# One transformer layer with paged decode: cached keys stored channel first, with homes of their own beside the values

## What is computed

```
z = h @ w_in                                   # 13 tiles of up to 512 columns, for all 320 tokens
# indexer: scores of the 8 new tokens of a sequence against its 1032 keys
ik_all = concat([cache_ik[page_table].reshape(db, 1024, 64), ik], 1)
scores = sum_h( relu(iq_h @ ik_all.T / 8) * w_h );  idx = top_k(scores, 256)
# attention of the same tokens over the chosen keys
s = q @ k_sel.T / 8;  p = softmax(s);  o = p @ v_sel     # k and v from cache_k, cache_v by page
# retention with a state per sequence; then three projections; then a mixture of 32 experts
x = x + gt1 * (merged @ w_o);   x = x + gt2 * moe(h2)
```

## Time and profile before

| | |
|---|---|
| median of 3 runs | 1524.77 us (1523.85 to 1530.13) |
| profiled execution | 1522.9 us, of which span 1520.9 us |
| PE busy | 1416.1 us, 93% |
| DVE, ACT, POOL busy | 465.1, 234.1, 81.1 us |
| HBM traffic | 483 MB read, 4 MB written |
| granted TensorE clock, mean | 0.978 of full |
| share of PE, of DMA in the chain that ended last | 34%, 35% |

### The profile page before, as it was taken

The page is one execution under the profiler, slowest core; times in us unless marked ns, Lnnn a source line. Parts: engine busy times, 40 slices in busy tenths (PEclk is TensorE's granted clock), DMA queues, the critical chain, the costliest instruction groups (busy, mean ns, idle before and its releaser), DMA issues.

```text
span 1520.9 us, 16634 instructions
## 1 busy us (share of the span) xinstructions
PE 1416.1 (93%) x6667; PEld 580.3 (38%) x6667; DVE 465.1 (31%) x993; ACT 234.1 (15%) x420; POOL 81.1 (5%) x71
## 2 busy tenths in 40 slices
PE   4899999998898779999999999999999999999993
PEld 2454555564443343333333333333333333333331
DVE  4233597653221241221211311221221131122124
ACT  1020232114202121111111111111111011011111
POOL 0200510231000020000000000000000000000000
PEclk8999999999999969999999999999999999999998
DMA  7532316437755439999999999999999999999991
GB/s 276 184 125 72 138 58 164 166 118 258 276 200 194 175 136 382 429 427 427 427 430 429 428 429 428 428 429 429 429 428 428 428 428 430 429 428 429 428 427 65
DMA packets 74042, 488.18 MB, mean 321 GB/s; under 512 B 6312, under 2 KB 16872, under 8 KB 48272
## 3 DMA queue, kind: packets, MB, share of 16 engines
q1 hardware_dynamic: 71488, 475.01, 76.4%
q0 software_dynamic: 1792, 10.49, 2.0%
q10 hardware_dynamic: 720, 2.10, 0.4%
HBM read 483.46 MB, written 4.08 MB: 321 GB/s over the span
## 4 chain that ended last, share of the span: by engine, by line
DMA 35%; PE 34%; DVE 2%; ACT 1%; issue 1%; POOL 0%; POOLq 0%; DVEq 0%; SPq 0%; ACTq 0%
DMA ring<-in_w_gate_up 35%; PE ps L1408 15%; PE ps L1449 5%; PE ps L865 2%; PE ps L866 2%; PE ps L1355 2%; PE ps L1386 1%; PE ps L869 1%; PE ps L1293 1%; PE ps L1401 1%; PE ps L1310 1%; PE ps L1316 0%; PE ps L1431 0%; PE ps L1363 0%; PE ps L1390 0%
## 5 line engine op out<-in xcount | busy, mean ns | idle before, releaser
L1408 PE MATMUL ps<-ring,z 128*64 128x512 f32 x2048 | 451.1, 595 | 20.9 <-DMA ring<-in_w_gate_up 20.9
L1408 PEld LDWEIGHTS ps<-ring,z 128*64 128x64 f32 x2048 | 142.2, 137 | 327.6 <-issue 277.8
L1449 PE MATMUL ps<-ring,z 128*64 128x512 f32 x1024 | 226.0, 594 | 0.0
L1985 DVE TENSOR_SCALAR actT<-ps 128x512 f32<-128x512 f32 x32 | 22.1, 692 | 647.3 <-PE ps L1408 647.3
L1449 PEld LDWEIGHTS ps<-ring,z 128*64 128x64 f32 x1024 | 72.0, 137 | 149.4 <-issue 145.1
L884 PE MATMUL ps<-ring,actT 128*128 128x512 f32 (+1 forms) x208 | 107.2, 597 | 3.3 <-DMA ring<-in_w_in 3.3
L885 PE MATMUL ps<-ring,actT 128*128 128x512 f32 (+1 forms) x208 | 104.7, 585 | 0.0
L1355 PE MATMUL ps<-z,actT 128*64 128x512 f32 x384 | 88.6, 596 | 1.3 <-DVE actT L1937 1.3
L1386 PE MATMUL ps<-z,aT 128*128 128x512 f32 x128 | 66.2, 619 | 1.7 <-ACT z L803 1.2
L1958 DVE TENSOR_TENSOR z<-z,ps 128x512 f32<-128x512 f32 x64 | 44.0, 688 | 61.3 <-PE ps L1386 61.2
L791 ACT ACTIVATE actT<-actT 128x512 f32<-128x512 f32 x32 | 20.1, 628 | 259.5 <-DVE actT L1985 259.5
(11 more groups left out here) (322 smaller groups left out, 1304.2 us busy)
## 6 DMA issues: line engine op xcount, KB each, us to landing
ring<-in_w_gate_up SPq DMA_DIRECT2D x128, 2048.0 KB, 23.4
ring<-in_w_down SPq DMA_DIRECT2D x64, 2048.0 KB, 20.6
ring<-in_w_ada SPq DMA_DIRECT2D x12, 2048.0 KB, 8.7
ring<-in_w_in SPq DMA_DIRECT2D x12, 2048.0 KB, 7.8
ring<-in_w_branch_b SPq DMA_DIRECT2D x2, 2048.0 KB, 10.6
ring<-in_w_out SPq DMA_DIRECT2D x2, 2048.0 KB, 10.7
ring<-in_state SPq DMA_DIRECT2D x8, 256.0 KB, 7.7
ret_sample<-ring SPq DMA_DIRECT2D x8, 256.0 KB, 7.5
```

Of the source, the lines that this page charges most:

```text
L1408: done = nc.tensor.matmul(bank(q // 2)[64 * (q % 2):64 * (q % 2) + 64, :], lhs, ring3[k // 2][:, (k % 2) * 2048 + q * BANK:(k % 2) * 2048 ...
L1449: done = nc.tensor.matmul(bank(2)[64 * q:64 * q + 64, :], lhs, ring3[4 + k // 4][:, (k % 4) * D + q * BANK:(k % 4) * D + (q + 1) * BANK], ...
```

## The change

The host now lays the caches out as `cache_kT` (page, channel, key), `cache_v` and `cache_ik` (page, channel, key), and passes the page numbers. Index keys are gathered by page, straight into `ikT`, 32 gathers of 64 KB in place of 8 of 256 KB. Attention keys are loaded by page from SP (sequences 0 to 5 during z tiles 10 to 12, sequence 6 in the attention) and from ACT (sequence 7): each page is a register load from `pt`, then a DMA of 64 KB with a row of 512 bytes for each channel. Keys and values have separate homes. POOL gathers the values alone, 512 KB a sequence, all after the last `new_state`. The transposes of keys and their copies go. The first pair's scores come before the wait for the rows' copies and the mask, and the modulation tile of a round follows directly on the values of the round before.

```diff
-        ikn = [scr(5332 + 1024 * i, 1024)... for i in range(PAIRS)]
-        kv_z = [z3[:, t, CRQ:CRG] for t in range(3)]
-        kv = [kv_z[0], kv_z[1], scr(5332, 2048), kv_z[2], scr(7380, 2048), scr(11476, 2048), scr(9428, 2048), kv_z[0]]
-        kT = [scr(2060, KEYS), scr(15316, KEYS)]
+        k_homes = [z3[:, 0, CRQ:CRG], z3[:, 1, CRQ:CRG], scr(5332, 2 * PAST), z3[:, 0, CRQ:CRG]]
+        v_homes = [z3[:, 2, CRQ:CRG], scr(11476, 2 * PAST), scr(7380, 2 * PAST), scr(9428, 2 * PAST)]
+        kT = [k_homes[b // 2][:, PAST * (b % 2):PAST * (b % 2 + 1)] for b in range(DB)]
...
+        def load_keys(q, b, first=0, last=NPAGES):
+            for n in range(first, last):
+                page = q.value_load(pt[0:1, b * NPAGES + n:b * NPAGES + n + 1], min_val=0, max_val=NPOOL - 1)
+                q.dma_start(kT[b][:, n * PAGE:(n + 1) * PAGE],
+                            a["cache_kT"][bass.ds(page, 1)].rearrange("a d s -> (a d) s")).then_inc(keys_here[b // 2], 16)
...
         @block.sync
-            load_z_tiles(10, 13)
+            sp.wait_ge(pr_here, 32)
+            load_z_tiles(10, 11)
+            sp.wait_ge(r_o, 1)
+            load_keys(sp, 0)
+            load_keys(sp, 1)
+            load_z_tiles(11, 12)
+            sp.wait_ge(r_o, 2)
+            load_keys(sp, 2)
+            load_keys(sp, 3)
+            load_z_tiles(12, 13)
             sp.wait_ge(retp_done, 1)
             sp.dma_start(a["ret_prompt"]...)
+            sp.wait_ge(r_o, 3)
+            load_keys(sp, 4)
+            load_keys(sp, 5)
             load_modulation(17, 4)
...
             load_modulation(19, 6)
+            sp.wait_ge(ssc2_done, 1)
+            load_keys(sp, 6)
             load_modulation(20, 7)
...
         @block.gpsimd
-            pool.wait_ge(h_done, 2)
-            for b in range(DB):
-                nc.gpsimd.indirect_dma_start(ikn[b // 2][:, :, b % 2, :].rearrange("p n d -> p (n d)"), None, rows,
-                                             bass.IndirectOffsetOnAxis(ap=irow[:, b:b + 1], axis=0)).then_inc(gathered[b // 2], 16)
+            pool.wait_ge(tile_done, 4)
+            for i in range(PAIRS):
+                for n in range(NPAGES):
+                    at = DB + i * NPAGES + n
+                    nc.gpsimd.indirect_dma_start(ikT[i][:, n * PAGE:(n + 1) * PAGE], None, rows,
+                                                 bass.IndirectOffsetOnAxis(ap=irow[:, at:at + 1], axis=0)).then_inc(gathered[i], 16)
...
             pool.wait_ge(ns_mm, 4)
-            gather_keys_values(3)
-            gather_keys_values(5)
-            pool.wait_ge(st_out[0], 64)
-            gather_keys_values(4)
-            pool.wait_ge(st_out[1], 64)
-            gather_keys_values(6)
-            pool.wait_ge(spv_done, 1)
-            gather_keys_values(7)
+            for b in range(DB):
+                if b in (4, 6):
+                    pool.wait_ge(st_out[b // 2 - 2], 64)
+                gather_values(b)
...
         @block.scalar
-            keys_out(0)
-            keys_out(1)
             for i in range(PAIRS):
-                if i + 1 < PAIRS:
-                    keys_out(2 * i + 2)
                 act.wait_ge(smx_done, i + 1)
...
-                if i + 1 < PAIRS:
-                    keys_out(2 * i + 3)
+                if i < 2:
+                    load_keys(act, 7, 4 * i, 4 * i + 4)
...
         @block.tensor
             for i in range(2):
-                prompt_steps(i, 0, 4)
-                index_transpose(2 * i)
-                prompt_steps(i, 4, KT)
-                index_transpose(2 * i + 1)
+                prompt_steps(i, 0, KT)
                 sample_steps(i)
...
             def sample_scores(i):
-                pe.wait_ge(kt_done, 4 * i + 4)
+                pe.wait_ge(keys_here[i], 32 * NPAGES)
...
             def sample_values(i):
                 pe.wait_ge(spt_done, i + 1)
+                for b in (2 * i, 2 * i + 1):
+                    pe.wait_ge(gathered[b], 16 * NPAGES + 16 if b < PAIRS else 16)
...
-            key_transpose(0)
-            key_transpose(1)
             sample_scores(0)
             for i in range(PAIRS):
-                if i + 1 < PAIRS:
-                    key_transpose(2 * i + 2)
                 if i:
                     pe.wait_ge(spt_done, i)
+                else:
+                    pe.wait_ge(rows_done, 6)
                 modulation_tile(17 + i, 3)
-                if i + 1 < PAIRS:
-                    key_transpose(2 * i + 3)
                 if i:
                     sample_rows(i - 1)
                 sample_prob_transposes(i)
...
         @block.vector
-            for i in range(PAIRS):
-                for h in range(2):
-                    dve.wait_ge(ikt_tr, 2 * i + h + 1)
-                    nc.vector.tensor_copy(ikT[i].rearrange("p (s n) -> p n s", n=8)[:, 4 * h:4 * h + 4],
-                                          bank(3 + 2 * (i % 2) + h).rearrange("p (n s) -> p n s", n=4)).then_inc(ikt_done, 1)
...
-            sample_top(1)
+            sample_top(2)
             new_state(2)
-            sample_top(1)
+            sample_top(2)
             new_state(3)
-            sample_top(2)
```

More of the change, by code:

```diff
@@ L284, in kern @@
         sa_tr, so_done, r_done, r_zero = sem("sa_tr"), sem("so_done"), sem("r_done"), sem("r_zero")
+        keys_here = [sem(f"keys_here{i}") for i in range(PAIRS)]
         gathered = [sem(f"gathered{b}") for b in range(DB)]
@@ L695, in _ @@
                     act.wait_ge(rows_tr, 2 * t + i + 1)
+                    b, at = ((5, 0), (6, 0), (7, 0), (3, 0), (4, 0), (4, 4 * NS))[2 * t + i]
                     nc.scalar.activation(rT[:, 4 * i:4 * i + 4, t * P:t * P + n],
-                                         bank((5, 0, 3)[t] + i).rearrange("p (k n) -> p k n", k=4)[:, :, 0:n],
+                                         bank(b)[:, at:at + 4 * n].rearrange("p (k n) -> p k n", k=4),
                                          ACT.Copy).then_inc(rows_done, 1)
[L700 to L708, removed]
             def sample_rows_out(i):
@@ L899, in sample_steps @@
                 last.then_inc(tile_done, 1)
-            def index_transpose(i):
-                pe.wait_ge(gathered[i], 32)
-                for h in range(2):
-                    if i >= 2:
-                        pe.wait_ge(ikt_done, 2 * (i - 2) + h + 1)
-                    for n in range(4):
-                        for j in range(2):
-                            last = nc.tensor.matmul(bank(3 + 2 * (i % 2) + h)[64 * j:64 * j + 64, n * P:(n + 1) * P],
-                                                    ikn[i][:, 4 * h + n, j, :], ident, start=True, stop=True)
-                    last.then_inc(ikt_tr, 1)
             def key_and_index_query_transposes():
                 pe.wait_ge(ikd_done, 1)
-                pe.wait_ge(ikt_done, 2 * PAIRS)
                 for t in range(3):
@@ L960, in sample_dots @@
                     pe.wait_ge(iw_done, 1)
+                pe.wait_ge(gathered[i], 16 * NPAGES)
                 for k in range(2):
@@ L1160, in _ @@
             for t in range(3):
[L1161 to L1162 removed]
                 n = TOK[t]
[L1164 to L1179 removed]
+                for i in range(2):
+                    if t == 0:
+                        pe.wait_ge(ns_done, 3)
+                    if t == 1 and i:
+                        pe.wait_ge(ns_done, 4)
+                    b, at = ((5, 0), (6, 0), (7, 0), (3, 0), (4, 0), (4, 4 * NS))[2 * t + i]
+                    for k in range(4):
+                        last = nc.tensor.transpose(bank(b)[:, at + k * n:at + (k + 1) * n],
+                                                   h2[0:n, t, (4 * i + k) * P:(4 * i + k + 1) * P], ident[0:n, 0:n])
+                    if t < 2:
+                        last.then_inc(rows_tr, 1)
+            last.then_inc(rows_tr, 2)
             def modulation_tile(n, b):
@@ L1201, in sample_scores @@
                     pe.wait_ge(z_done, NZT)
-                    pe.wait_ge(masks_done, 1)
-                    pe.wait_ge(rep_done, DB)
-                    pe.wait_ge(vnew_here, 16 * DB)
-                for k, w in ((0, BANK), (1, BANK), (2, DS)):
+                blocks = ((0, BANK), (1, BANK), (2, DS))
+                for k, w in blocks:
                     if i and k == 2:
@@ L1209, in sample_scores @@
                         b = 2 * i + h
+                        keys = kT[b][:, k * BANK:k * BANK + w] if k < 2 else kTn[:, SEQ + b * DS:SEQ + (b + 1) * DS]
                         nc.tensor.matmul(bank(k)[NS * h:NS * h + NS, 0:w], z3[:, 2, CQ + b * NS:CQ + (b + 1) * NS],
-                                         kT[h][:, k * BANK:k * BANK + w], start=True, stop=False)
+                                         keys, start=True, stop=False)
+                if i == 0:
+                    pe.wait_ge(masks_done, 1)
+                    pe.wait_ge(rep_done, DB)
+                    pe.wait_ge(vnew_here, 16 * DB)
+                for k, w in blocks:
                     for h in range(2):
```

(10 more changed lines are left out.)

51 lines of the change are left out of this document (15 added, 36 removed).

## The result

The changed kernel takes 1531.87 us (median of 5 runs, 1529.27 to 1537.61) against 1524.77; the ratio is 1.0043, with a 95% interval of 1.0028 to 1.0059. So it is slower by 0.4%, and the forecast of 1504.5, 1500.5 to 1514, failed in size and in sign. The profiled execution took 1531.87, its span 1529.6; by the forecast the span would have been 1520.9 - 20.3 = 1500.6. Three marks of PE split the 29.0 us between forecast and measured span.

A forecast was written before the change was run, and what follows sets the result against it. PE was taken as the limit in the z tiles, PE with ACT in the sample attention, weights in the expert stage; 7.6 + 8.3 + 4.4 = 20.3 us off 1522.9 gives 1502.6, as median 1504.5 us, range 1500.5 to 1514.

The forecast's parts named there:

- Step 1: Z tiles: the index transposes, 128 PE instructions in four blocks of 1.90 us, go; 7.6 us gained.
- Step 5: POOL's 32 index gathers, about 42 to 82 us, beside the load of z tile 2: price 0, bound 4 us.
- Rival B: Index pages in 512-byte rows delay z tile 2 or the first tiles by up to 4 us: 1508.5; chance 0.08.
- Step 2: Sample attention, rows' transposes to first probabilities: these come at 353.4 in place of 369.27, 8.3 us of it won here.
- Step 3: Sample attention's rounds: 9.3 us each, three of them 27.9, without the wait for a key copy; 4.4 us gained.
- Rival A: Attention becomes fed by DMA, tiles 18 and 19 late: two stalls of 3 us, 1510, up to 1514; chance 0.17.
- Step 4: After the attention: projections, router and experts keep their distances; gain or loss 0.
- Step 6: SP's queue, key page loads between z tile loads: about 1.2 us a page, 19 a pair of sequences; price 0.
- rival C: SP's queue overflows with 48 pages, deciding from 2.0 to 2.1 us a page; 1547 at 3.0; chance 0.05.

## Why the prediction was wrong

**Step 1, index transposes, held.** Without the crawl the rows' transposes begin at 344.43 to 344.91, where 344.8 was forecast.

**Step 5, POOL, failed, and made the sign.** It counted the gathers right (40 us, from 42 to 82) and priced them at 0 with a bound of 4, because it looked for what they could take from others in DMA bandwidth alone. Their cost was 18.4 us, in which PE waited for no semaphore and issued next to nothing, and step 1's sentence "No later wait in the z tiles depends on anything but PE" was false in it. That bound was over four times too small, as the nearest row was a series of 8 gathers, which hurts nobody, and four times the length isn't four times a row. Rival B had the right place, z tile 2 late, by another mechanism and with 4 of the 18. The waits named as its mark, for `in_w_in` at tile 2, did not come.

The Trainium skill, "Runtime: NRT & Kernel Launch", section "Instruction fetch mechanics", describes each engine's instruction memory as a queue refilled in blocks of 16 KiB by DMA ahead of need, which mostly hides the fetch. Packets of 0.02 MB at fixed places in PE's program agree with the first part. Waits marked "issue" inside one loop make a fetch that is not hidden the nearest reading of the crawl, and it would contradict the second; but it is argued, not shown. The crawl begins ahead of the packet's place (182 against 204 matmuls), goes on behind the packet in the run with the small multiplications, and a packet came in the middle of a series of 8. So it is shown that an unbroken series of gathers makes PE crawl; what it takes from PE stays open.

**Step 2, first probabilities, held**: 8.85 us after the rows' start against 8.6, with the waits for the rows' copies and for DVE's copy that it named.

**Step 3, the rounds, held as PE's own time and failed as a forecast.** An undisturbed round is 8.76 (forecast 9.3). Rival A, which had 0.17, came true: tile 18 was issued at 363.4 and wanted at 378.0, 14.6 later (A had 14.9), and landed after 19.4. "At worst 15.6" was a tile beside 3 MB of gathers too, and I took the same company to give the same delay; why it gave 4 us more was not separated. Two more things were mis-sized. A asked for two stalls of 3 us, it was one of 4.9; and the half clock behind a stall, some 4 us more (the first two rounds are 8.96 above two undisturbed ones, the wait is 4.93), had no term at all. That pacing won back 5.8 of the 7.6 shows the gathers as the cause.

**Step 4 held** to 1441 us within 0.4; of the other 2.6, 1.6 are a clock that differs in the same way between other kernels' executions, and 1.0 in one wait for a weight stays unexplained.

**Step 6, SP's queue, held**: 17.1 us for 16 pages, 1.07 each against 1.2, and rival C with its 2.0 was far off. One issue of sequence 6 took 6.6 us with the queue full, and nobody waited for it. In the run with index pages by SP the queue did cost a stall; the cover counted, not the price of a page.

The sum of the plan was right: with both losses taken out, the changed kernel runs at 1504.6, and the forecast was 1504.5. That they agree to 0.1 is luck: the four executions spread from 1500.9 to 1507.5. By stretches the profiled one has 344.31 against 344.8 and 43.05 against 42.95, but 1111.3 against 1112.85, and inside the attention the first probabilities came 7.87 us after the rows' start (forecast 8.6) and the rounds took 8.78, 10.16 and 9.79 (forecast 9.3 each), errors that cancel.

## What to carry to other kernels

Keep series of GpSimd gathers short (8 in a row, some 10 us, cost nothing in any run), and put a wait for another engine's progress between two of them; if PE shows waits for "issue" inside one loop while the DMA engines are idle, look at what POOL is doing. Where transfers of one stage are issued together, hold the ones needed last behind the arrival of those needed first. A price of 0 for "the same work in more pieces" needs a row with as many pieces in a row, or an upper bound by the whole length of the series.

## What the runs showed of the hardware that was not expected

- While POOL issues indirect gathers back to back (0.94 us each and 0.30 between), PE can come down to a matmul or two in 2 us, with no semaphore to wait for. It began 19 to 26 us into an unbroken series and lasted until 3 to 6 us after its last gather. 8 in a row (10 us) cost nothing, 16 nothing once and 6.6 us once, 32 cost 18.4 us in one kernel and 26.4 in the other. Pauses of 0.8 us behind every four helped in part. What the gathers take from PE is not shown.
- Arithmetic on POOL for the same length does not do this, but held a DVE operation on SBUF for 9.39 us in place of 0.38. The Trainium skill, "SBUF — State Buffer", section "SBUF: two separate sides", has the two engines share a port pair as an exclusive lock for one instruction, the loser blocked. The trace agrees that it blocks, and shows more: POOL's operations take 1.23 us each here (31.88 for 26), so if it was this lock, DVE lost it to some seven of them in a row. DVE's next five operations, beside POOL's eight small multiplications from 87.7 on, took 0.37 to 0.41 each.
- A load of a page chosen by a register costs SP 1.07 us in a series (17.1 for 16).
